# A depthwise convolution of 31 taps in 32x32 tiles of the PE array, and the attention steps beside it in another order

## The reference, cut to what matters

```
def conv_mixer(u, w, b, gn_g, gn_b):          # u (1, 256, 512): values and gates
    a, gt = jnp.split(u, 2, axis=-1)
    z = a * jax.nn.sigmoid(gt)                # 256 channels
    zp = jnp.pad(z, ((0, 0), (CONV_WIDTH - 1, 0), (0, 0)))          # CONV_WIDTH = 31
    y = lax.conv_general_dilated(zp, w[:, None, :], (1,), 'VALID',
                                 feature_group_count=CONV_CH) + b   # each channel by itself
    ...                                       # group norm over 4 groups of 64 channels, gains, silu
```

## Time and profile before

| | |
|---|---|
| three runs, us | 1075.69, 1074.46, 1073.70 (median 1074.46) |
| profiled execution, its time, us | 1073.52 |
| its span, us | 1071.7 |
| mean granted clock of TensorE | 0.997 |
| busy, share of the span | TensorE 98%, DVE 74%, ACT 65%, POOL 7% |
| DMA over the span | 176 GB/s |

### The profile page before, as it was taken

How to read it: one execution, slowest core, us unless ns; L and a number is a source line. 1 busy time by engine, 2 the same in 40 slices (tenths; PEclk the granted TensorE clock), 3 DMA queues, 4 the chain that set the end, 5 groups by cost and what they waited for, 6 DMA issues and landing times.

```text
span 1071.7 us, 21582 instructions
## 1 busy us (share of the span) xinstructions
PE 1048.7 (98%) x7982; PEld 951.8 (89%) x7982; DVE 789.1 (74%) x1317; ACT 691.5 (65%) x1247; POOL 75.5 (7%) x113
## 2 busy tenths in 40 slices
PE   8999999999999999999999999999999999999997
PEld 8999788999999899988899999998989988888886
DVE  6856667877777796567687777777787769568995
ACT  7675666655555777568565555567975558457884
POOL 1002500000000000242030000000000000100000
PEclk9999999999999999999999999999999999999999
DMA  7643114656665455511456656564543326968992
GB/s 270 193 150 116 43 63 167 194 189 183 182 191 188 124 181 158 164 35 61 138 170 201 190 176 185 187 180 133 160 141 114 104 104 212 389 228 331 374 359 82
DMA packets 51689, 187.82 MB, mean 175 GB/s; under 512 B 6176, under 2 KB 6336, under 8 KB 51360
## 3 DMA queue, kind: packets, MB, share of 16 engines
q1 hardware_dynamic: 49104, 178.95, 51.0%
q0 software_dynamic: 2512, 7.88, 2.1%
HBM read 184.71 MB, written 3.67 MB: 176 GB/s over the span
## 4 chain that ended last, share of the span: by engine, by line
PE 83%; ACT 7%; DVE 6%; DMA 2%; issue 2%; POOLq 0%; POOL 0%; SPq 0%; DVEq 0%; ACTq 0%
PE bank L1850 23%; PE bank L1851 22%; PE bank L1852 22%; PE bank L1951 4%; DMA ring<-wtiles 1%; PE bank L1935 1%; ACT w L2334 1%; DVE x L2700 1%; DVE act L2683 1%; PE bank L2144 1%; DVE w L2659 1%; PE bank L2015 1%; DVE sq L2691 1%; PE bank L758 1%; PE bank L954 1%
## 5 line engine op out<-in xcount | busy, mean ns | idle before, releaser
L2659 DVE TENSOR_TENSOR w<-ring,w 128x1024 fp32r<-128x1024 f32 x240 | 293.0, 1224 | 98.1 <-ACT w L2334 97.5
L1850 PE MATMUL bank<-act,w 128*128 128x256 f32 x1136 | 324.3, 286 | 2.8 <-DVE w L2659 2.5
L1851 PE MATMUL bank<-act,w 128*128 128x256 f32 x1136 | 321.4, 283 | 0.0
L1852 PE MATMUL bank<-act,w 128*128 128x256 f32 x1136 | 321.3, 283 | 0.0
L2334 ACT ACTIVATE w<-ring 128x1024 fp32r<-128x1024 f32 x240 | 252.8, 1055 | 69.7 <-PE bank L1852 47.8
L1850 PEld LDWEIGHTS bank<-act,w 128*128 128x128 f32 x1136 | 217.6, 192 | 7.6 <-issue 3.6
L1851 PEld LDWEIGHTS bank<-act,w 128*128 128x128 f32 x1136 | 217.7, 192 | 1.7
L1852 PEld LDWEIGHTS bank<-act,w 128*128 128x128 f32 x1136 | 217.7, 192 | 0.0
L2969 DVE SCALAR_TENSOR_TENSOR region<-bank,pf,region 128x255 f32<-128x255 f32 (+1 forms) x176 | 84.8, 482 | 33.9 <-ACT region L2616 23.7
L1850 PE MATMUL bank<-w,hid 128*128 128x512 f32 x206 | 80.8, 392 | 0.0
L2616 ACT ACTIVATE region<-bank,pf 128x256 f32<-128x256 f32 x88 | 49.5, 562 | 48.3 <-PE bank L1852 40.5
(11 more groups left out here) (482 smaller groups left out, 1964.5 us busy)
## 6 DMA issues: line engine op xcount, KB each, us to landing
ring<-wtiles SPq DMA_DIRECT2D x240, 512.0 KB, 3.6
ring<-etiles SPq DMA_DIRECT2D x33, 512.0 KB, 5.1
act_raw<-etiles SPq DMA_DIRECT2D x33, 512.0 KB, 5.4
sq<-etiles SPq DMA_DIRECT2D x22, 512.0 KB, 5.3
cst<-etiles SPq DMA_DIRECT2D x8, 512.0 KB, 5.5
region<-packp POOLq DMA_DIRECT2D x4, 512.0 KB, 4.4
cst<-consts SPq DMA_DIRECT2D x1, 1176.5 KB, 10.8
x<-xt SPq DMA_DIRECT2D x2, 512.0 KB, 5.4
```

Of the source, the lines that this page charges most:

```text
L1850: t.matmul(out_, still[:, 0], moving[:, 0], start=first, stop=False)
L1851: t.matmul(out_, still[:, 0], moving[:, 1], start=False, stop=False)
L1852: return t.matmul(out_, still[:, 1], moving[:, 0], start=False, stop=last)
L2659: v.tensor_tensor(w_lo[:, s, :], ring[:, s, :], w_hi[:, s, :].bitcast(F32), ALU.subtract).then_inc(lo_ready, 1)
```

## The change

1. The six tiles of taps go (240 tiles become 234), and with them the hi and lo parts of c_z and DVE's taps. Token tiles 21 and 22 become 20 and 21; within_rows and within_keys move into token tile 20.
2. conv_part does all 62 taps in fp32 matmuls (not parted) of 32x32 tiles: row group r takes channels 32r to 32r + 31 of a half j, column group q stands for a half (q // 2) and for the even or odd tap of a pair (q % 2). For a pair of taps that is 16 matmuls of 256 columns (8 for the last); four that follow each other have four row groups and four column groups. Row group r adds up in bank 6, 0, 1 or 5. 248 matmuls in all, at steps 23 (80), 24 (80), 25 (48) and 26 (40), ahead of what these steps did behind their tile. The first one waits for c_z, the taps' loads, GLA's copied states, df_sm 7 (bank 6 read by the masks) and the evacuations of the last tokens.
3. conv_fold adds the even and odd taps and puts the channels in order: ACT copies the four banks (conv_copy), 8 matmuls of 128x32 with a 0/1 matrix, ACT adds the bias. It stands behind the second half of out_part(0), which is cut into its two halves of tokens; the means (L901) move behind out_part(1), and the spreads ahead of out_part(1) don't wait for the convolution any more. Attention's lengths move from bank 0 to bank 7.
4. The taps, 2 x 512 KB, are loaded by POOL's DMA queue over buffers of block one, the first when block one's tiles are done, the second behind lr_done. The constants grow by 64 columns.
5. In steps 20 to 23 masked(4) to masked(7), difference(1) and difference(2) stand ahead of DVE's refill, and weigh(3) to weigh(6) ahead of ACT's evacuation and refill.

The core of the diff:

```diff
-U_CONV, U_DQ, U_OG, U_DVA, U_GV, U_DVB, U_STEPS = 2, 6, 14, 16, 18, 21, 28
-TAP_TILES = 6
-U_TAPS = (20, 23, 24, 25, 26, 27)[:TAP_TILES]
+U_CONV, U_DQ, U_OG, U_DVA, U_GV, U_DVB, U_STEPS = 2, 6, 14, 16, 18, 20, 28
...
+PAIRS_OF_TAPS = (CW + 1) // 2
+CONV_STEPS = {23: (0, 5), 24: (5, 10), 25: (10, 13), 26: (13, PAIRS_OF_TAPS)}
+CONV_BANKS = (6, 0, 1, 5)
...
+            def conv_part(first, end):
+                if first == 0:
+                    pe.wait_ge(cz_ready, 2)
+                    pe.wait_ge(taps_in, 32)
+                    pe.wait_ge(st_copied, 2)
+                    pe.wait_ge(df_sm, 7)
+                    pe.wait_ge(u_evac, evacuated(U_DVB + 1))
+                for s in range(first, end):
+                    for turn_ in range(4):
+                        for r in range(4):
+                            q = (r + turn_) % 4
+                            j, tap = q // 2, 2 * s + q % 2
+                            if tap >= CW:
+                                continue
+                            rows_, outs = slice(32 * r, 32 * r + 32), slice(32 * q, 32 * q + 32)
+                            still = tap_parts[s // 8][rows_, s % 8 * P + 32 * q:s % 8 * P + 32 * q + 32]
+                            mm = t.matmul(bank[CONV_BANKS[r]][outs, 0:S], still, c_z[rows_, j, tap:tap + S],
+                                          start=s == 0, stop=tap + 2 >= CW)
...
+            def conv_fold():
+                pe.wait_ge(cp_copied, 4)
+                for j in range(2):
+                    for r in range(4):
+                        mm = t.matmul(bank[1][32 * r:32 * r + 32, j * S:(j + 1) * S], cc("fold32", j, 32), c_part[:, r, :],
+                                      start=True, stop=True)
+                mm.then_inc(cp_done, 1)
...
-            out_part(0)
+            out_part(0, (0,))
+            pe.wait_ge(cp_copied, 1)
+            pe.wait_ge(hn_std, 2)
+            out_part(0, (1,))
+            conv_fold()
             pe.wait_ge(hn_inv, 2)
-            pe.wait_ge(cy_ready, 2)
             for j in range(DFH):
                 spread(bank[4 + j // 2][:, j % 2 * S:j % 2 * S + S], o_inv[:, 2 * j:2 * j + 2]).then_inc(hn_row, 1)
+            out_part(1)
+            pe.wait_ge(cy_ready, 2)
             for j in range(2):
                 mm = t.matmul(bank[0][:, j * S:(j + 1) * S], bd64, c_y[:, j, :], start=True, stop=True)
             mm.then_inc(cm_done, 1)
-            out_part(1)
...
             for u in range(U_STEPS):
                 src = bank[u % 4]
+                i = u - U_DVA - 1
+                if 3 <= i < 7:
+                    weigh(i)
...
+                i = u - U_DVA
+                if 4 <= i < 8:
+                    masked(i)
+                    if u in (20, 22):
+                        difference((u - 18) // 2)
                 if u in AT and u != U_CONV + 4:
                     refill(AT[u])
...
         def second_pool(pool):
+            pool.wait_ge(tile_done, T2)
+            pool.dma_start(tap_parts[0][:], ctaps[0]).then_inc(taps_in, 16)
+            pool.wait_ge(lr_done, 1)
+            pool.dma_start(tap_parts[1][:], ctaps[1]).then_inc(taps_in, 16)
             pool.wait_ge(mix_lo, DEPTH * KD + KD)
```

More of the change, by code:

```diff
@@ L183, in evacuated @@
 def evacuated(u):
-    return sum(i not in CONV_VALUES and i not in U_TAPS for i in U_TILES if i <= u)
+    return sum(i not in CONV_VALUES for i in U_TILES if i <= u)
 def columns(*widths):
@@ L313, in block_program @@
         gid = ctx.enter_context(nc.sbuf_tensor("gid", [P, NG], mybir.dt.int32))
+        places["hid"] = -(-nc.sbuf_base // 32) * 32
         hid_both, hid_hi, hid_lo = split("hid", 2, S)
         thin_both, thin_w_hi, thin_w_lo = split("thin", KD * 64)
-        cz_hi = hid_both[:].rearrange("p b q s -> p (b q s)")[:, 0:2 * (S + CW - 1)].rearrange("p (j s) -> p j s", j=2)
-        cz_lo = thin_both[:].rearrange("p b n -> p (b n)")[:, 0:2 * (S + CW - 1)].rearrange("p (j s) -> p j s", j=2)
+        assert nc.sbuf_base == places["hid"] + 4 * 2 * 1024 and 4 * S == KD * P
+        tap_parts = [nc.alloc_sbuf_tensor_at(f"taps{i}", [P, 1024], F32, offset=places["hid"] + i * 4096) for i in range(2)]
         last_both, last_hi, last_lo = (a_[..., 0:S] for a_ in (thin_both, thin_w_hi, thin_w_lo))
@@ L417, in block_program @@
         c_sq = ar.take(2, S)
+        c_part = g_pr[:, 0:4, :]
         d_raw, d_sq = h, sq
@@ L747, in second_tensor @@
                     project_tokens(n, n % SLOTS, half, [bank[pair % 2 * 2 + c] for c in range(NT)], between_tokens.get(u))
-                elif u in U_TAPS:
-                    if u == U_TAPS[0]:
-                        pe.wait_ge(cz_low, 2)
-                        pe.wait_ge(st_copied, 2)
-                    tile_in(n)
-                    for i in range(KD):
-                        tap = U_TAPS.index(u) * KD + i
-                        j, w = PE_TAPS[tap]
-                        first, last = w == 0, tap == len(PE_TAPS) - 1 or PE_TAPS[tap + 1][0] != j
-                        out_, weights = bank[5][:, j * S:(j + 1) * S], wblock(n % SLOTS, i)
-                        t.matmul(out_, weights[:, 0], cz_hi[:, j, w:w + S], start=first, stop=False)
-                        t.matmul(out_, weights[:, 0], cz_lo[:, j, w:w + S], start=False, stop=False)
-                        mm = t.matmul(out_, weights[:, 1], cz_hi[:, j, w:w + S], start=False, stop=last)
-                        if i == KD - 1:
-                            mm.then_inc(tile_done, 1)
-                        if u == U_WITHIN and i == 4:
-                            within_rows()
-                        if u == U_WITHIN and i == KD - 1:
-                            within_keys()
+                elif u in CONV_STEPS:
+                    conv_part(*CONV_STEPS[u])
                 if u == 2:
@@ L871, in second_tensor @@
                         pe.wait_ge(df_o, 2 * j + 2)
-                        mm = lengths(bank[0][:, 2 * j:2 * j + 2], d_osq[:, j, :], ones[:, 0:1])
+                        if j == 0:
+                            pe.wait_ge(df_sm, 8)
+                        mm = lengths(bank[7][:, 2 * j:2 * j + 2], d_osq[:, j, :], ones[:, 0:1])
                         if j == DFH - 1:
@@ L1056, in gate, with conv_copy @@
                 a.activation(c_sg[:, j, :], bank[(CONV_VALUES[j] + 1) % 4][:, 0:S], ACT.Sigmoid).then_inc(u_evac, 1)
[L1058 to L1061 removed]
+            def conv_copy(r):
+                a.activation(c_part[:, r, :], bank[CONV_BANKS[r]][:, 0:S], ACT.Copy).then_inc(cp_copied, 1)
             def lengths_root(src, dst):
@@ L1129, in second_scalar @@
                     act.wait_ge(hn_sum, 2)
-                    a.activation(o_rms[:], bank[0][:, 0:2 * DFH], ACT.Sqrt, bias=eps, scale=1.0 / P).then_inc(hn_std, 1)
-                    a.activation(c_y[:, 1, :], bank[5][:, S:2 * S], ACT.Identity, bias=pb_("convb", 1)).then_inc(cy_ready, 1)
+                    a.activation(o_rms[:], bank[7][:, 0:2 * DFH], ACT.Sqrt, bias=eps, scale=1.0 / P).then_inc(hn_std, 1)
+                    for r in range(1, 4):
+                        conv_copy(r)
+                    act.wait_ge(cp_done, 2)
+                    for j in range(2):
+                        a.activation(c_y[:, j, :], bank[1][:, j * S:(j + 1) * S], ACT.Identity, bias=pb_("convb", j)).then_inc(cy_ready, 1)
                 if u in AT:
@@ L3129, in shape_constants @@
     put("onecol", np.tile(np.arange(33) == 1, (P, 1)))
+    put("fold32", np.concatenate([(i[:, None] // 64 == q) & (i[:, None] % 32 == np.arange(32)[None, :]) for q in range(2)], axis=1))
     put("halfcols", i[:, None] // 64 == np.arange(32)[None, :])
```

83 lines of the change are left out of this document (26 added, 57 removed).

## The result

| | before | after |
|---|---|---|
| median, us | 1074.46 (1072.20 to 1076.76, 9 runs) | 1077.64 (1075.91 to 1079.38, 9 runs) |
| ratio to before | 1 | 1.0030, 95% interval 1.0021 to 1.0039 |
| span of the profiled execution, us | 1071.7 | 1075.8 |

What follows compares the result with a forecast made beforehand. TensorE, busy 98% of the span, was taken as the bound. Projection 3.8 us earlier, less 0.9 for the fold, left 2.9; less 1.6 for the clock, 1.3 earlier: 1074.46 to 1073.2 us, range 1070.0 to 1078.0.

Steps and rivals of the forecast that it cites:

- the price of the 248 small matmuls: Convolution on TensorE: 496 records at 16 ns each, 7.9 us in all.
- The bounds: Limits on the convolution's matmul time: 6.7 us with sixteen tiles at once, 26.8 us with only four.
- DVE's walk: DVE from the second scores to masked(6): convolution can't start until 823.4 us, with 3.6 us of TensorE idle in front.
- The clock: Around the convolution's start: half clock for about 3.2 us after idle time, costing 1.6 us, bounds 0 and 2.4.
- The end of the stretch: Output projection's start: set by the GLA mix at 840.3 instead of 844.1 us, 3.8 us earlier.
- The fold: Behind out_part(0): 8 added matmuls, 16 records of 58 ns, 0.9 us; ACT's four copies lie beside out_part(0).
- Behind the mixer: Everything after the changed stretch, router and experts included: only shifts along, no change of its own.
- The order of masks and splits: DVE's masks and differences moved ahead of splits: takes nothing off the wait by itself.
- The transfers: DMA loads of taps on POOL's queue and 32 KB more constants: taken as 0 us.
- A: Rival, the forecast itself: sixteen tiles at once and the clock falls for a while; 1073.2 us; chance 0.36.
- C: Rival: convolution's tiles can't be issued fast enough, 28 ns a record, 14.0 us; 1077.7 us in all; chance 0.13.
- D: Rival: only four convolution tiles run at once, 54 ns a record, 26.8 us; 1090.5 us in all; chance 0.12.

Runs made afterwards that it cites:

- e2: Changed kernel with the convolution's matmuls at 128 columns in place of 256, half the tokens left out; 1074.66 us, one run.
- e3: Changed kernel with the convolution's first row group in bank 3 instead of 6, waiting for the second turn's copy, not masked(6); 1073.19 us.
- e4: Changed kernel with within_blocks moved behind masked(6) on DVE; 1073.08 us.
- e1: Changed kernel with 7 extra whole-array matmuls ahead of the third scores and 16 ahead of the convolution's wait, filling idle time; 1076.15 us.
- e6: Changed kernel without the fold's 8 matmuls, three of ACT's four copies and the wait for the fold; 1076.01 us.
- e8: Changed kernel with masks, differences and exponentials put back behind refill, the old order; 1078.28 us, ratio 1.0039.
- e11: Changed kernel with the 16 matmuls of a pair of taps ordered by row group; 1080.37 us, one run.
- e5: As e3, with the convolution's four parts one step earlier, the first 80 matmuls ahead of the third scores; 1072.37 us.
- e7: Kernel before the change with only the new order of masks, differences and exponentials; 1073.84 us, ratio 1.0001.
- e9: As e5, with the last 40 matmuls at step 27 and six whole-array matmuls ahead of GLA's spreads; ACT's first copy later; 1070.07 us.
- e12: As e4, with all 248 matmuls in one stretch at step 23; 1082.86 us.
- e10: As e5, with 6 extra whole-array matmuls ahead of GLA's spreads and 12 ahead of the output projection; 1073.82 us.

## Why the prediction was wrong

The forecast was 1073.2 us, 1.3 earlier than before, with a range from 1070.0 to 1078.0; the time is 1077.64, 3.2 later, slower, for which the chance stood at 0.24. **The step that failed is the price of the 248 small matmuls**, "I take 16 ns, 7.9 us". They take 3.32 + 3.32 + 2.06 + 1.92 = 10.6 us at the full clock, 2.7 more. 1.5 of it is the distance of starts, 19.0 ns in place of 16 (496 x 3); the rest is that each of the four stretches has an end of its own, some 0.3 us until its last records are through, which the sum by starts left out. With this term alone put right the sum gives 1.4 us later in place of 1.3 earlier, and e2 shows that it reaches the projection in full. The bounds held (6.7 to 26.8 us), the value lay too near the lower one: the 64x64 row showed starts of matmuls whose work is a quarter as long.

Point by point:

- DVE's walk was right: convolution at 11.2 from the scores by the walk, 11.46 measured; 3.63 us idle in front, 3.6 predicted; ended by masked(6) as said. e3 and e4 show that this wait is what the tiles of steps 20 and 23 turned into.
- The clock was right: 4.69 - 3.32 = 1.4 us lost in this trace (1.6 predicted), 1.0 by the ratio of e1, which the intervals alone don't tell from none. But it isn't the same in each execution, so that the size fitted this one is partly luck: e6, e8 and e11 have the convolution behind as much idle time and stood 6.8 to 10.2 us at half clock there, where the changed kernel's profiled run stood 3.4. Among the nine runs of the changed kernel the three of 1078.76 to 1079.38 us have a mean granted clock of 0.992 to 0.993, the six of 1075.91 to 1077.70 one of 0.995 to 0.996.
- The end of the stretch: the projection waits for the mix chain as walked (0.70 us idle behind L2675). It starts 1.05 us later than before where 2.2 earlier was forecast (3.8 less the clock's 1.6); of the 3.3 us between, 2.7 are the small matmuls, less 0.2 for the clock, 0.2 DVE, and 0.6 the matmuls right behind three of the stretches: in the chains the first two of the values take 0.42 us behind the third and the fourth stretch where they took 0.22 before, and the transposes behind the second 0.48 where they took 0.33. That is a cost of the stretches too, and the prediction has no term for it.
- The fold was under-priced: 0.9 us predicted, 1.35 from projection to additions in the trace (27.93 against 26.58), 1.4 by e6's trace and 1.7 by its ratio.
- Behind the mixer I expected nothing, and the trace has 0.5 us more (201.6 against 201.0 from the additions to the end), with one fall of the clock in each, at 877.8 before and at 903.0 after. The traces without one there (e5, e6, e7, e9, e12) take 199.9 to 200.0. So the 0.5 us go with where the clock fell; why it fell there isn't shown.
- The order of masks and splits "takes nothing off this by itself": e7 and e8 show no change of the time that is clear of the noise, but in e8's trace the old order starts the convolution 1.0 us later. The transfers cost nothing that shows: the constants' load with its 32 KB more takes 10.8 us as before, and step 20's scores start at 813.35, at 813.37 in e7, which has no loads of taps by POOL.

Sum in the trace: 1.05 + 1.35 + 0.54 = 2.9 us, and 3.2 by the medians. Of the rivals, A's mechanism came true with another size. C's time (1077.7) came out by accident: records are 19 ns apart, not 28. D was wrong: four tiles at once, at 54 ns, would have taken 26.8 us.

The Trainium skill ("TensorE: Matmul & The Clock Gate", "Measured speedup vs the span model") gives sixteen packed tiles 10.6 times the rate of one; the trace shows 217 / 19.0 = 11.4 from start to start and 217 x 496 / 10.6 us = 10.2 with the ends. The estimate of 10.1 us by it was nearer to the 10.6 measured than my 7.9. The floor of some 25 ns between starts that the Trainium skill gives ("TensorE: Matmul & The Clock Gate", "Wait — 56ns, not 53.3ns?") doesn't hold here: 19.0 ns, and 12.9 in e2.

## What to carry to other kernels

Work that is taken off the bounding engine in front of a wait is no gain: find what the wait is for, and move work into it (e5, e9) or shorten the chain that ends it (e3, e4), before counting it. Price a new form of instruction by whole stretches with their ends, not by the distance of two starts, and when only one nearby row exists, work out how far its price must be off to turn the sign: here 1.3 of 7.9 us were enough. Idle time on TensorE can have a second price, the clock behind it; filling it pays only as long as the filling is shorter than the wait (e10). Whether useful work is a better filling than as much that is thrown away was not tried.

## What the runs showed of the hardware that was not expected

- Records of fp32 matmuls of 32x32 tiles and 256 columns start 19.0 ns apart in the mean over a stretch of 160: 6 to 8 ns in the first 32, mostly 16 to 17 behind them, with pauses of 118 to 192 ns, in the end one after every 34 records. With 128 columns the mean is 12.9 ns. The order of the sixteen tiles made no difference (e11, one run).
- The first whole-array matmuls behind a stretch of small ones take 0.15 to 0.20 us longer than they did before (0.42 against 0.22, 0.48 against 0.33).
- In one stretch of 496 records TensorE stopped for 1.37 us at record 483 and 0.44 at 355, with nothing in the profile that it waited for (e12). Whether instructions came too late was not tried.
- The same idle time of 3.6 us went with 3.4 us at half clock in one execution and 6.8 in another (changed kernel, e6), 1.23 us in front of the convolution with none in e4 and 6.8 us in e12, and 0.89 us in front of GLA's spreads with 10.2 us in e5.
